# RWKV-7 recurrence of one layer: state and read-out products in 64x64 tiles of both heads, decayed state added on VectorE, scores and tokens of two blocks issued together

## The chip, the cores and the metric

The program runs on one core of one Trainium2 chip. The metric is the device time of one execution in microseconds. Three runs of the kernel before gave 1727.79, 1728.28 and 1729.55 us, median 1728.28.

## The reference

One layer of a streaming encoder on 1024 tokens of width 1024: a mixing stage (8 heads of latent attention beside 8 heads of RWKV-7), a memory cross-attention with 256 memory tokens, a squared-ReLU MLP of width 4096 and a last RMSNorm, all in float32. The change touches the RWKV-7 recurrence alone. Per head (64 channels) and token the reference does:

```python
def step(state, inp):
    rt, wt, kt, vt, at, bt = inp
    sa = jnp.einsum('bhvk,bhk->bhv', state, at)
    state = state * wt[:, :, None, :] + sa[..., None] * bt[:, :, None, :] + vt[..., None] * kt[:, :, None, :]
    return state, jnp.einsum('bhvk,bhk->bhv', state, rt)
```

After it each head is normalised, a bonus term sum(r k r_k) v is added and a gate multiplies the result. The rates w, a and the gate come from low-rank products of the projected input.

## The kernel before

**Stages.** The execution runs the input projection, attention with pieces of other work between its heads (to about 442 us), then the recurrence loop (first solve at 463.25, last output at 717.0 us), then the memory values, the output projection, cross-attention and the MLP, which are long rows of full matmuls. Every stage is written out as one instruction order per engine, with semaphores (`Steps` objects name each event) between the engines. A wait holds up all that stands behind it on its engine.

**The recurrence loop.** Heads go in pairs: channels of head 0 of the pair on partitions 0 to 63, of head 1 on 64 to 127. A round is one pair (`p`, 0 to 3). The 1024 tokens are 16 chunks (`c`) of 64, two chunks are a block (`w`, 8 of them), two blocks a group (`g`, 0 to 3 in a round). In a group TensorE does, for its own two blocks: `solve` (L1361), the inverse of the chunk's triangular system times two right sides, gives P and G; `local` and `other_r` (L1372, L1411) give what a chunk reads from itself and its matrix for reading the state; `carry` (L1418) gives the matrix by which the state moves over a chunk, to which VectorE adds the diagonal decay (`mt`, L2748) that GpSimd built as diagonal matrices (`dg`, L902). Then, for k = 0 to 3, `state` (L1437, copied out by VectorE at L2758) and `outputs` (L1449) of one chunk each. `state` and `outputs` contract over 128 partitions: the state with an identity under it, and the transition matrix with the additive part under it, so that each is one 128-row, 64-column product per head (L1445, L1458).

Between these stand, for the next group: the doubling of the inverse (`double_q` L1334 for k = 0 and 2, `double_z` L1347 for k = 1 and 3, masked or added by VectorE at L2721 and L2730), `scores` of one block for k = 0 and 1 (L1290, masked by VectorE at L2604), `tokens` of one block for k = 2 and 3 (L1312: three 128x128 transposes and one 128x128 product, copied by ScalarE at L1941 to L1944), and after k = 3 `a_v` of both blocks (L1325, copied at L1949).

**Work beside it.** `beside(p, s)` puts slot `s` of 44 per round into the order: `prep(p+1, s)` makes the next round's inputs and `post(p-1, s-22)` finishes the last round's output. Group g has slots 11g+4 to 11g+6 before k = 0 and two slots for each k (11g+7+2k and the next; the first before and the second after `scores` or `tokens`). Slots that matter here, with their lines:
- 0 to 3: four low-rank products on TensorE (L1208), each followed by a tanh on ScalarE (L1882, L1886), all through one PSUM bank; slot 3 also has three VectorE passes.
- 5 to 7: squares on ScalarE (L1892), two block sums on TensorE (L1211), each followed by a logarithm (L1897).
- 10, 11: exponentials W, kf and Wi on ScalarE (L1903, L1905, L1908). 14 to 17: VectorE passes nkk (L2512, which needs kf), at (L2517), b and bt (L2522, L2526), kt (L2529).
- 18, 19: products `al` (L1256), masked by VectorE (L2539), which SyncE stores to DRAM and loads back as 16x16 blocks (L689, L693).
- 26 to 30: 15 substitution steps on those blocks, two small VectorE instructions each (L2562, L2565), then `xt` (L2568), stored and loaded again for the inverses.
- 28, 29 and 37 to 39: the statistics and the gate of the round before (L1211, L1208, L2588 to L2598). 33, 34: the bonus sums (L1211, L2574).

Slots 0 to 3 of the next round fall after k = 2 and 3 of group 3. In round 3 there is no next round, and ScalarE and VectorE prepare the memory tokens instead (L1976 to L2000, L2632).

## Time and profile before

| what | value |
|---|---|
| three runs | 1727.79, 1728.28, 1729.55 us |
| profiled execution, its own time | 1724.08 us |
| its span, first to last instruction | 1722.0 us |
| mean granted TensorE clock | 0.985 |
| busy share: TensorE, VectorE, ScalarE, GpSimd | 96%, 65%, 51%, 45% |
| recurrence loop, first solve to last output | 463.25 to 717.0 us |

The span is the time between the first and the last instruction on the core; the execution's own time has 2.1 us around it. A TensorE row of the timeline merges neighbouring instructions of one line; its duration runs from the first start to the modelled end of the last. A float32 product shows as two matmul instructions, a transpose as one. PEclk is the granted clock, 1.00 for 2.4 GHz and 0.50 for 1.2 GHz.

### The profile page before, as it was taken

To read this page: it belongs to the slowest core of one execution; us is meant where nothing else is said; L and a number is where in the kernel's file an instruction comes from. 1 tells how busy PE (TensorE), PEld (TensorE's weight loads), DVE (VectorE), ACT (ScalarE), POOL (GpSimd) and SP (SyncE) were. 2 spreads that over 40 slices of the span, in tenths; PEclk is the share of its full clock that TensorE was granted. 3 is DMA by queue.
4 is the path that set the end of the run, shared out by engine and by line. 5 is a ranking of instruction groups with operands and counts; after the bars stand their busy time and mean duration, and the time that the engine had idled before them with its cause. 6 is when DMAs were issued, how large, how long until landed. Compare 5 with 4: busy or idle time off the path is not lost.

```text
span 1722.0 us, 30291 instructions
## 1 busy us (share of the span) xinstructions
PE 1653.9 (96%) x11840; PEld 1272.0 (74%) x11840; DVE 1115.8 (65%) x1728; ACT 869.9 (51%) x1687; POOL 768.4 (45%) x555
## 2 busy tenths in 40 slices
PE   8999999998989888899999999999999999999997
PEld 6676777745666667688977667788888888888886
DVE  7744343435576675633687769887758866784788
ACT  5323333345334444611453467776667566666763
POOL 4120212011111122313393257968768695867771
PEclk9999999979899999999999999999999999999999
DMA  6010010001121214332302003020212202120202
GB/s 241 25 37 22 25 47 1 22 6 31 33 36 42 53 24 128 136 110 73 111 25 74 1 1 98 19 80 26 74 30 69 72 28 92 31 74 25 74 1 98
DMA packets 82841, 94.45 MB, mean 55 GB/s; under 512 B 53776, under 2 KB 56336, under 8 KB 82704
## 3 DMA queue, kind: packets, MB, share of 16 engines
q1 hardware_dynamic: 82704, 92.56, 17.3%
q8 instruction: 93, 1.52, 0.4%
q14 instruction: 44, 0.36, 0.1%
HBM read 82.57 MB, written 9.98 MB: 54 GB/s over the span
## 4 chain that ended last, share of the span: by engine, by line
PE 79%; DVE 10%; ACT 4%; issue 3%; DMA 2%; POOL 2%; SPq 0%; DVEq 0%; ACTq 0%; POOLq 0%
PE PS L1707 41%; PE PS L1034 8%; PE PS L969 5%; PE PS L1135 3%; PE PS L1174 2%; PE PS L1153 2%; PE PS L1208 2%; PE PS L1663 2%; PE PS L1641 1%; PE PS L1211 1%; PE PS L1499 1%; POOL sa L917 1%; PE PS L1343 1%; DMA sc_s<-a_dram 1%; PE PS L1445 1%
## 5 line engine op out<-in xcount | busy, mean ns | idle before, releaser
L1707 PE MATMUL PS<-memr,wsp 128*128 128x512 f32 x1488 | 358.3, 391 | 1.0 <-DVE memr L2877 1.0
L1707 PEld LDWEIGHTS PS<-memr,wsp 128*128 128x128 f32 x1488 | 278.8, 188 | 63.7 <-DVE memr L2877 3.0
L932 POOL TENSOR_TENSOR wsp<-sa,wsp 128x512 fp32r<-128x512 f32 x120 | 167.5, 1399 | 166.0 <-ACT wsp L2135 165.8
L1707 PE MATMUL PS<-memr,wraw_r 128*128 128x512 f32 x744 | 180.5, 391 | 0.0
L1707 PEld LDWEIGHTS PS<-memr,wraw_r 128*128 128x128 f32 x744 | 139.4, 188 | 30.9 <-DVE memr L2877 0.6
L1707 PE MATMUL PS<-tmp_r,wsp 128*128 128x512 f32 x564 | 148.3, 397 | 2.5 <-DVE tmp_r L2877 2.2
L2877 DVE TENSOR_TENSOR memr<-PS,memr 128x512 fp32r<-128x512 f32 x185 | 126.1, 682 | 34.9 <-ACT PS L2173 34.6
L1034 PE MATMUL PS<-xn,wsp 128*128 128x512 f32 x576 | 147.5, 403 | 0.9 <-DVE tmp L2350 0.7
L969 PE MATMUL PS<-xn,wsp 128*128 128x512 f32 x576 | 132.5, 391 | 5.0 <-DVE xn L2313 3.7
L2895 DVE TENSOR_TENSOR H<-PS,H 128x512 f32<-128x512 f32 x160 | 108.1, 686 | 44.7 <-PE PS L1707 28.0
L823 POOL CAST wsp<-wraw 128x1024 fp32r<-128x1024 f32 x24 | 26.5, 1106 | 240.1 <-PE PS L1034 115.9
L1034 PEld LDWEIGHTS PS<-xn,wsp 128*128 128x128 f32 x576 | 105.6, 190 | 33.8 <-issue 13.8
L1842 ACT ACTIVATE H<-PS,mst 128x128 f32<-128x128 f32 (+3 forms) x64 | 47.4, 741 | 164.2 <-DVE mst L2442 164.2
L969 PEld LDWEIGHTS PS<-xn,wsp 128*128 128x128 f32 x576 | 107.8, 188 | 29.8 <-issue 4.9
L1707 PEld LDWEIGHTS PS<-tmp_r,wsp 128*128 128x128 f32 x564 | 105.4, 188 | 29.7 <-DVE tmp_r L2877 4.0
L2164 ACT CAST memr<-sa 128x512 fp32r<-128x512 f32 x114 | 70.2, 616 | 109.7 <-PE PS L1707 80.0
L932 POOL TENSOR_TENSOR wraw_r<-sa,wraw_r 128x512 fp32r<-128x512 f32 x64 | 89.0, 1394 | 53.5 <-ACT wraw_r L2135 53.5
L917 POOL TENSOR_TENSOR sa<-sa 128x512 f32<-128x512 f32 x64 | 91.7, 1434 | 34.9 <-DMA sa<-in_weights_dram 33.0
L2173 ACT COPY PS<-sa 128x512 f32<-128x512 f32 x175 | 101.9, 582 | 3.2 <-DVE con_r L2877 1.8
L2442 DVE TENSOR_REDUCE mst<-PS 128x1 f32<-128x128 f32 (+3 forms) x64 | 48.1, 753 | 85.1 <-PE PS L1138 85.0
L932 POOL TENSOR_TENSOR wsp<-sbx,wsp 128x512 fp32r<-128x512 f32 x66 | 88.6, 1345 | 11.9 <-ACT wsp L2135 11.8
L2821 DVE TENSOR_TENSOR sa<-sa 128x512 f32<-128x512 f32 x80 | 88.4, 1108 | 6.6 <-ACT sa L2114 6.6
(382 smaller groups left out, 3393.2 us busy)
## 6 DMA issues: line engine op xcount, KB each, us to landing
sa<-in_weights_dram SPq DMA_DIRECT2D x40, 512.0 KB, 4.3
wraw<-in_weights_dram SPq DMA_DIRECT2D x24, 512.0 KB, 3.8
sa<-in_weights_dram SPq DMA_DIRECT2D x48, 256.0 KB, 2.8
H<-in_x_dram SPq DMA_DIRECT2D x16, 512.0 KB, 7.7
sbx<-in_weights_dram SPq DMA_DIRECT2D x32, 256.0 KB, 2.9
H<-in_weights_dram SPq DMA_DIRECT2D x8, 512.0 KB, 7.3
out_dram<-sbx SPq DMA_DIRECT2D x16, 256.0 KB, 2.1
a_dram<-H SPq DMA_DIRECT2D x16, 128.0 KB, 2.5
```

What stands on the lines that cost most here:

```text
L917: nc.gpsimd.tensor_tensor(out, a, b, op).then_inc(W_SUM.sem, W_SUM.one(name))
L932: nc.gpsimd.tensor_tensor(w[:, 1, :], w_source(g), w[:, 0, :].bitcast(F32), ALU.subtract).then_inc(mw_rest, 1)
L969: last = nc.tensor.matmul(PS[:, bank + half, :], wsp[:, k, kt, a, :], src[:, at, b, HALF * half:HALF * half + HALF], start=(i == 0 and (a, ...
L1034: last = nc.tensor.matmul(PS[:, bank, :], wsp[:, u % 2, kt, a, :], xn[:, kt, b, HALF * half:HALF * half + HALF], start=(kt == 0 and (a, b) ...
L1135: nc.tensor.matmul(PS[:, b + part, 0:n], mQ[:, win(q)], mK[:, HALF * part:HALF * part + n], start=True, stop=(part < q // 4))
L1707: last = nc.tensor.matmul(PS[:, bank_of(g), :], w[:, a, win(k)], x[:, b, :], start=(k == 0 and (a, b) == (0, 0)), stop=(k == ROWS - 1 and ...
L2164: nc.scalar.copy(x_split_of(d)[:, 0, :], x_source(d)).then_inc(mx_head, 1)
L2173: nc.scalar.copy(PS[:, PS_BANKS + d % 2, :], x_source(d)).then_inc(mx_staged, 1)
L2442: m(nc.vector.tensor_reduce(mNeg[h % 2][:, q:q + 1], two(2 * (q % 2))[:, 0:P * (q + 1)], AX_X, ALU.max, negate=True), f"m{h}_{q}")
L2821: nc.vector.tensor_tensor(out, a, b, op).then_inc(X_SUM.sem, X_SUM.one(name))
L2877: nc.vector.tensor_tensor(x[:, 1, :], source, x[:, 0, :].bitcast(F32), ALU.subtract).then_inc(mx_rest, 1)
L2895: out(nc.vector.tensor_tensor(tile, a, b, ALU.add), f"{kind}{part}_{v}")
```

## The change

Head h of a pair keeps to partitions 64h to 64h+63 all through the recurrence. The state is one tile of 128x64 for each chunk (both heads, no identity under it), the transition matrix has no diagonal and no additive part, and both `state` and `outputs` are 64x64 products, one for each head. The additive part goes straight into the PSUM bank of the new state with `given` (four 64x64 products for each chunk, issued one chunk ahead), and `state` adds its product to it. VectorE then makes the new state with one scalar_tensor_tensor: old state times the chunk's decay (a column for each channel) plus the PSUM tile. GpSimd's diagonal matrices, the `mt` addition on VectorE and the selection products `from_r` are gone: ScalarE copies the transition matrices (`mt`) and the local outputs (`ly`), VectorE adds r to the local reads (`r`) and the local outputs to the read-out (`y`), which ScalarE only copied before. Scores and tokens of both blocks of a group are issued together, for k = 0 and k = 1, with one masking instruction for both; the tokens are 32 products of 64x64 with the identity as moving operand instead of transposes; `a_v` comes for k = 2. Their ScalarE copies stand at the same places: four token copies between the two slots of k = 1, the `a_v` copy between those of k = 2. The setting up of the loop loses VectorE's 64x2048 identity copy and five memsets but one, and its filler products are placed differently. DMA issues are the same; some of SyncE's, GpSimd's and ScalarE's waits name the new events.

In the cut below the lines that it removes are left out (they are in the listing above), and of the new order of each engine what matters; 8 columns of indent are taken off.

```diff
@@ -1287,60 +1274,69 @@
...
+    def scores(p, g):
...
+        for s in range(2):
+            w, at = 2 * g + s, 192 * s
+            for h, c in QUADS:
+                rows = slice(HD * h, HD * h + HD)
+                nc.tensor.matmul(PS[chunk(c), h, at:at + CH], rB[i][rows, win(w)][:, chunk(c)],
+                                 rAR[i][rows, w, 1, chunk(c)], start=True, stop=True)
+            for h, c in QUADS:
+                rows = slice(HD * h, HD * h + HD)
+                last = nc.tensor.matmul(PS[chunk(c), h, at + CH:at + 3 * CH].rearrange("p (a n) -> p a n", a=2),
+                                        proj[rows, T_K + p, win(w)][:, chunk(c)], rAR[i][rows, w, :, chunk(c)],
+                                        start=True, stop=True)
+        last.then_inc(L_PE.sem, L_PE.one(f"sc{p}_{g}"))
+    def tokens(p, g):
+        i = p % 2
+        if g == 0:
             r_at(P_POOL, f"bh_{p}")
...
+        r_at(L_DVE, f"sc{p}_{g}")
+        for s in range(2):
+            w, at = 2 * g + s, 256 * s
+            for h, c in QUADS:
+                rows = slice(HD * h, HD * h + HD)
+                nc.tensor.matmul(PS[chunk(c), h, at + 192:at + 256], proj[rows, T_V + p, win(w)][:, chunk(c)],
+                                 con[rows, C_CV + HD * h:C_CV + HD * h + HD], start=True, stop=True)
+            for k, src in enumerate((rAR[i][:, w, 0, :], rBh[i][:, win(w)], rKh[i][:, win(w)])):
+                for h, c in QUADS:
+                    rows = slice(HD * h, HD * h + HD)
+                    last = nc.tensor.matmul(PS[chunk(c), h, at + CH * k:at + CH * k + CH],
+                                            src[rows, chunk(c)], ident[rows, rows], start=True, stop=True)
+        last.then_inc(L_PE.sem, L_PE.one(f"tok{p}_{g}"))
...
@@ -1350,114 +1346,84 @@
...
+    def quad(out, h, c, left, right, start, stop):
+        return nc.tensor.matmul(PS[HD * h:HD * h + HD, out[0], out[1]:out[1] + CH], left, right, start=start, stop=stop)
+    def cols(h):
+        return slice(HD * h, HD * h + HD)
+    def carry(p, g):
+        for s in range(2):
+            r_at(L_ACT, f"pg{p}_{2 * g + s}")
+            for h, c in QUADS:
+                quad((c, CH * s), h, c, rPG[s][chunk(c), h, 0:HD], rBKs[g % 2][chunk(c), s, 0, cols(h)], True, True)
+            for h, c in QUADS:
+                quad((c, P + CH * s), h, c, rPG[s][chunk(c), h, HD:P], rSC[s][chunk(c), h, 0, :], True, False)
+            for h, c in QUADS:
+                last = quad((c, P + CH * s), h, c, rVs[g % 2][chunk(c), s, h, :], rSC[s][chunk(c), h, 2, :], False, True)
+        last.then_inc(L_PE.sem, L_PE.one(f"mn{p}_{g}"))
+    def reads(p, g):
+        for s in range(2):
+            for h, c in QUADS:
+                last = quad((2 + c, CH * s), h, c, rPG[s][chunk(c), h, 0:HD], rSC[s][chunk(c), h, 0, :], True, True)
+        last.then_inc(L_PE.sem, L_PE.one(f"lr{p}_{g}"))
+    def given(p, c):
...
+        e = c // 4 % 2
+        for k, right in enumerate((rPG[s][:, :, HD:P], rVs[e][:, s])):
+            for h in range(2):
+                last = quad((5 - n, 0), h, n, rBKs[e][chunk(n), s, k, cols(h)], right[chunk(n), h, :], k == 0, False)
+        last.then_inc(L_PE.sem, L_PE.one(f"n{p}_{c}"))
     def state(p, c):
...
+        if c % 4 == 0:
+            r_at(L_ACT, f"mt{p}_{c // 4}")
+        r_at(L_PE, f"n{p}_{c}")
         if c >= 1:
             r_at(L_DVE, f"st{p}_{c - 1}")
...
         for h in range(2):
...
+            last = quad((5 - c % 2, 0), h, h, rMT[cols(h), c % 2, c // 2 % 2, :], rST[cols(h), c, :], False, True)
         last.then_inc(L_PE.sem, L_PE.one(f"st{p}_{c}"))
     def outputs(p, c):
...
+        if c % 4 == 0:
+            r_at(L_DVE, f"r{p}_{c // 4}")
         if c >= 1:
             r_at(L_DVE, f"st{p}_{c - 1}")
...
         for h in range(2):
...
+            last = quad((4 + c % 2, P + CH * (c // 2 % 2)), h, h, rST[cols(h), c, :],
+                        rR[cols(h), c % 2, c // 2 % 2, :], True, True)
+        last.then_inc(L_PE.sem, L_PE.one(f"o{p}_{c}"))
     def beside(p, s):
@@ -1577,33 +1546,26 @@
             for w in ab:
                 solve(p, w)
             beside(p, t + 4)
...
+            carry(p, g)
+            reads(p, g)
             beside(p, t + 5)
...
+            given(p, 4 * g)
             beside(p, t + 6)
             for k in range(4):
                 c = 4 * g + k
...
                 if c < NC - 1:
                     state(p, c)
...
+                outputs(p, c)
                 first, second = places(g, k)
                 if more:
                     for n in range(2):
                         (double_z if k % 2 else double_q)(k // 2, *following(p, g, n))
+                if k < 3 and c < NC - 2:
+                    given(p, c + 1)
                 beside(p, first)
...
+                if more and k < 3:
+                    (scores, tokens, a_v)[k](*group_after(p, g))
                 beside(p, second)
...
@@ -1934,20 +1894,19 @@
...
+    def tokens(p, g):
+        tok = PS[:, 0:2, :].rearrange("p h (s k n) -> p s k h n", s=2, k=4)
+        r_at(L_PE, f"tok{p}_{g}")
+        nc.scalar.copy(rVs[g % 2], tok[:, :, 3]).then_inc(L_ACT.sem, L_ACT.one(f"vz{p}_{g}"))
+        nc.scalar.copy(rAGs[:, :, :, 0:HD], tok[:, :, 0]).then_inc(L_ACT.sem, L_ACT.one(f"ag{p}_{g}"))
+        for s, name in enumerate(("ba", "bk")):
+            nc.scalar.copy(rBKs[g % 2][:, s].rearrange("p k (h n) -> p k h n", h=2), tok[:, s, 1:3]).then_inc(
+                L_ACT.sem, L_ACT.one(f"{name}{p}_{g}"))
...
@@ -2066,28 +2023,24 @@
             more = g < NW // 2 - 1 or p < PAIRS - 1
             for w in ab:
                 r_at(L_PE, f"pg{p}_{w}")
...
+                nc.scalar.copy(rPG[w % 2].rearrange("p h n -> p (h n)"), PS[:, 2 + w % 2, 0:256]).then_inc(
                     L_ACT.sem, L_ACT.one(f"pg{p}_{w}"))
             beside(p, t + 4)
...
+            r_at(L_PE, f"mn{p}_{g}")
+            nc.scalar.copy(rMT.rearrange("p c s n -> p c (s n)"), PS[:, 0:2, 0:P]).then_inc(
+                L_ACT.sem, L_ACT.one(f"mt{p}_{g}"))
+            if p or g:
+                r_at(L_DVE, f"y{p}_{g - 1}" if g else f"y{p - 1}_{NW // 2 - 1}")
+            nc.scalar.copy(rY.rearrange("p c s n -> p c (s n)"), PS[:, 0:2, P:2 * P]).then_inc(
+                L_ACT.sem, L_ACT.one(f"ly{p}_{g}"))
             beside(p, t + 5)
             beside(p, t + 6)
             for k in range(4):
                 first, second = places(g, k)
...
                 beside(p, first)
...
+                if more and k in (1, 2):
+                    (tokens, a_v)[k - 1](*group_after(p, g))
                 beside(p, second)
...
@@ -2741,30 +2687,39 @@
         for g in range(NW // 2):
             ab, t = (2 * g, 2 * g + 1), 11 * g
             more = g < NW // 2 - 1 or p < PAIRS - 1
...
+            beside(p, t + 4)
+            r_at(L_PE, f"lr{p}_{g}")
+            nc.vector.tensor_tensor(rR, PS[:, 2:4, 0:P].rearrange("p c (s n) -> p c s n", s=2),
+                                    rAR[p % 2][:, ab[0]:ab[0] + 2, 1, :].rearrange("p s (c n) -> p c s n", c=2),
+                                    ALU.add).then_inc(L_DVE.sem, L_DVE.one(f"r{p}_{g}"))
+            beside(p, t + 5)
             beside(p, t + 6)
             for k in range(4):
                 c = 4 * g + k
                 if c < NC - 1:
                     r_at(L_PE, f"st{p}_{c}")
...
+                    if c == 0:
+                        r_at(P_ACT, f"wt_{p}")
+                        dve.wait_ge(rp_dve, 2)
+                    else:
+                        r_at(L_DVE, f"st{p}_{c - 1}")
+                    nc.vector.scalar_tensor_tensor(rST[:, c + 1], rST[:, c], rWT[p % 2][:, c:c + 1],
+                                                   PS[:, 5 - k % 2, 0:CH], ALU.mult, ALU.add).then_inc(
                         L_DVE.sem, L_DVE.one(f"st{p}_{c}"))
                 first, second = places(g, k)
                 if more:
                     for n in range(2):
                         (added_z if k % 2 else masked_q)(k // 2, *following(p, g, n))
+                if k == 3:
+                    r_at(L_PE, f"o{p}_{c}")
+                    r_at(L_ACT, f"ly{p}_{g}")
+                    nc.vector.tensor_tensor(
+                        proj[:, T_R + p, 256 * g:256 * g + 256].rearrange("p (s c n) -> p c s n", s=2, c=2),
+                        PS[:, 4:6, P:2 * P].rearrange("p c (s n) -> p c s n", s=2), rY,
+                        ALU.add).then_inc(L_DVE.sem, L_DVE.one(f"y{p}_{g}"))
                 beside(p, first)
...
+                if more and k == 0:
+                    masked_scores(*group_after(p, g))
                 beside(p, second)
```

## Rows read from the trace of the kernel before

**Rows 1.** The page: its header and TensorE's busy time and share.
```profile
span 1722.0 us, 30291 instructions
...
PE 1653.9 (96%) x11840; PEld 1272.0 (74%) x11840; DVE 1115.8 (65%) x1728; ACT 869.9 (51%) x1687; POOL 768.4 (45%) x555
```

**Rows 2.** Busy time of stretches of the loop, with granted clock and DMA.
```profile
core 0: us, PE busy (x) PEld busy (x) DVE busy (x) ACT busy (x) POOL busy (x), PEclk, DMA share, GB/s
561.00:580.20 19.20, 17.01 (x314) 11.82 (x312) 14.51 (x50) 8.71 (x18) 2.99 (x5) 0.91 0.20 30
628.40:647.30 18.90, 15.72 (x314) 10.96 (x310) 14.10 (x50) 8.71 (x18) 2.92 (x5) 1.00 0.25 33
679.50:692.30 12.80, 11.32 (x306) 9.60 (x302) 8.20 (x21) 6.00 (x17) 5.44 (x4) 1.00 0.02 4
```

**Rows 3.** Timeline of TensorE: start, us, line, count, idle before.
```profile
463.25 1.97 PE L1368 MATMUL PS<-sc_s,H 64*64 64x128 f32 x16
...
600.97 0.70 PE L1425 MATMUL PS<-sc_s 64*64 64x64 f32 x26
...
603.74 0.34 PE L1458 MATMUL PS<-sc_s,tmp 128*64 128x64 f32 x4
...
604.23 0.68 PE L1343 MATMUL PS<-H 64*64 64x64 f32 x16
...
605.90 0.36 PE L1305 MATMUL PS<-sa 64*64 64x64 f32 x8
...
606.41 0.39 PE L1445 MATMUL PS<-tmp,ssum 128*64 128x64 f32 x3
...
609.50 0.33 PE L1318 MATMUL PS<-con,sa 128*128 128x128 f32 x1
609.66 0.27 PE L1319 MATMUL PS<-con,sa 128*128 128x128 f32 x1
...
612.87 0.45 PE L1330 MATMUL PS<-sc_s,sc_w 64*64 64x64 f32 x8 [0.42 <-ACT sc_s L1944]
613.15 1.19 PE L1368 MATMUL PS<-sc_s,H 64*64 64x128 f32 x16
...
620.14 1.15 PE L1256 MATMUL PS<-sa 64*64 64x64 f32 x32 [0.45 <-DVE H L2539]
```

**Rows 4.** Line L1425: shortest, median and longest ns of one instruction.
```profile
L1425 PE MATMUL PS<-sc_s x768: 218/218/267, 466.5 to 711.1; 64*64 64x64 f32 x192
```

**Rows 5.** The chain that ended last, inside round 2: start, us, what.
```profile
590.67 1.07 PE PS L1208 x2
...
596.39 1.14 PE PS L1208 x2
...
604.91 1.07 PE PS L1211 x2
...
606.62 1.28 ACT L1903
607.91 1.06 ACT sa L1903
608.97 0.94 ACT sa L1905
...
611.01 0.27 ACT sc_s L1942
...
611.62 1.23 DVE sa L2512
...
616.55 0.70 DVE ssum L2748
...
623.79 3.59 DMA a_dram<-H
...
639.57 0.38 DVE sc_s L2568
```

**Rows 6.** Timeline of VectorE: one masking of scores.
```profile
608.54 0.56 DVE L2604 TENSOR_TENSOR sc_w<-PS,con 128x384 f32<-128x384 f32 x1
```

More of the change, by code:

```diff
@@ L119 @@
 POST = 22
-RP_SET = 6
 SPLITS = ((10, 4), (14, 2))
@@ L1325, in a_v @@
[L1325 to L1332 removed]
+                if p or g:
+                    r_at(L_ACT, f"ly{p}_{g - 1}" if g else f"ly{p - 1}_{NW // 2 - 1}")
@@ L1334, in double_q, with a_v @@
+            def a_v(p, g):
+                r_at(L_ACT, f"bk{p}_{g}")
+                for h in range(2):
+                    for s in range(2):
+                        for c in range(2):
+                            last = nc.tensor.matmul(PS[chunk(c), s, HD * h:HD * h + HD], rSC[s][chunk(c), h, 1, :],
+                                                    rVs[g % 2][chunk(c), s, h, :], start=True, stop=True)
+                last.then_inc(L_PE.sem, L_PE.one(f"akv{p}_{g}"))
             def double_q(lv, p, w):
@@ L1404, in from_r @@
-            def from_r(p, w, h, c):
-                rows = slice(HD * h, HD * h + HD)
-                return nc.tensor.matmul(PS[0:HD, 2 + 2 * (w % 2) + c, CH * h:CH * h + CH],
-                                        con[rows, C_SEL + CH * h:C_SEL + CH * h + CH],
-                                        rAR[p % 2][rows, w, 1, chunk(c)], start=False, stop=(h != c))
-            def other_r(p, w):
-                r_at(L_PE, f"lo{p}_{w}")
-                for h in range(2):
-                    last = from_r(p, w, h, 1 - h)
-                last.then_inc(L_PE.sem, L_PE.one(f"ry{p}_{w}"))
@@ L1556, in attention_end @@
                     pair_factors(PAIRS - 1, s - 6)
-            for stage in (scores, tokens, a_v):
-                for w in range(2):
-                    if stage is scores and w or stage is tokens and not w:
-                        keep_busy(2 + w, 2 * P)
-                    stage(0, w)
-            pe.wait_ge(rp_dve, RP_SET)
+            scores(0, 0)
+            for bank in (2, 3):
+                keep_busy(bank, 2 * P)
+            tokens(0, 0)
+            keep_busy(4, HALF)
+            a_v(0, 0)
+            pe.wait_ge(rp_dve, 2)
             for bank in (2, 4, 3):
@@ L2055, in _ @@
                     values(h // 2 + 1)
[L2057 to L2060 removed]
+            tokens(0, 0)
+            a_v(0, 0)
             for s in range(4):
```

310 lines of the change are left out of this document (78 added, 232 removed).

## The prediction

> **What bounds the kernel now.** I read the page first: TensorE is busy 96% of a span of 1722.0 us [rows 1]. That share misleads in the loop, because a matmul's row lasts until its modelled end while the next ones already start. So I took the loop (254 us, 16 groups) by stretches [rows 2]: a group takes 12.8 us where nothing stands beside it and 19.2 where substitution does. Then the timeline of TensorE in round 2, for what each piece occupies from its start to the next start, and last the chain of waits in the same round, for what the next round's inputs need. The reader is to see that TensorE streams nearly without gaps, while a second chain (ScalarE, VectorE, DMA) runs just as long beside it. In round 2 it holds the end at four places [rows 5]:
> - slots 0 to 3, a product and a tanh in turn through one bank, 1.91 us each ((596.39-590.67)/3);
> - the block sum that ends at 605.98, the table load and exponentials (606.62 to 609.91), then four VectorE passes from 611.62 until `mt` at 616.55;
> - the trip of the blocks to DRAM and back from 623.79 and the substitution until 639.95;
> - TensorE for the rest, among it the 7.3 us from there to 647.3, where group 3 begins [rows 2].
>
> **TensorE, part by part.** In four quadrants an instruction costs (0.70-0.22)/25 = 19 ns [rows 3, 4]; on the two diagonal quadrants (0.68-0.22)/15 = 31 ns; with both column halves but one row half (L1256) (1.15-0.22)/31 = 30 ns [rows 3].
> - `state` and `outputs` of a chunk: 8 instructions, 0.49 us (603.74 to 604.23). As 64x64 on the diagonal: 8 x 30 ns = 0.24. Saves 0.25, 1.0 a group.
> - `local`, `other_r` and `carry`: 112 instructions a group become 64, all in four quadrants: saves 48 x 19 ns = 0.9.
> - `given`: 32 new instructions a group. No row shows it; between 19 ns and an unpipelined 218 [rows 4] the nearest is L1256, same row half, so 30 ns: adds 0.95.
> - scores: 0.51 a block now (605.90 to 606.41). Sorted by size, 8 x 19 + 8 x 28 (double columns) = 0.38: saves 0.25 a group.
> - tokens: three transposes and a product for a block come to 5 x 0.11 plus 0.05 for the change of mode (0.16 to the second transpose, then 0.11). 32 small instructions are 0.61. Even; 1.3 us a group either way.
> - `a_v`: its waits for the token copies (0.42 idle before L1330, beside 0.2 under the last row's end) go twice, 1.2 a group. `mt` no longer comes through VectorE: about 0.6.
>
> Together 3.0 us a group. If TensorE alone set the end, that would be 16 x 3.0 = 48 us. It doesn't.
>
> The Trainium skill speaks against `given`: by TensorE: Matmul & The Clock Gate (Part 3, What overlaps and what doesn't) a weight load overlaps a running matmul only when its row group differs, and `given` keeps to one row half. Row L1256 does the same and still runs at 30 ns, so the sum keeps that price; by the rule `given` would run one by one (a rival below).
>
> **The other engines.** VectorE loses `mt` (0.70 [rows 5]) and gets `r` and `y`, 128x256 from PSUM; between a masking of 128x384 (0.56 [rows 6]) and zero, by their third less columns, 0.4 each. The two maskings become one of double width: 2 x 0.56 less one fixed part of 0.16 = 0.96. The new state by scalar_tensor_tensor, 0.25 for a copy of 0.27. Even. ScalarE copies fewer and wider, 0.27 each for 256 columns [rows 5]. GpSimd loses 32 instructions that nothing waited long for; their absence is costed at nothing, under the `carry` products. SyncE issues the same DMAs.
>
> **What moves, round 2 walked through.** The price is in the order on ScalarE. Token copies stood after slots 10 and 11; now they stand before slot 10, and they wait for all token products.
> 1. The squares of slot 5 start once `carry` is copied: 0.9 less of products and one wait for products less (estimated 0.15), so 1.05 earlier. The block sum of slot 7 ends at 604.93 instead of 605.98.
> 2. TensorE then does scores 0.8, a chunk 0.25, doubling 0.95, `given` 0.25, tokens 1.3: 608.5. Four copies: 609.6. Only now the table load and exponentials, 1.28+1.06+0.94: kf at 612.9, before at 609.91. **3.0 later.**
> 3. Wi (0.95) and the `a_v` copy behind it end at 614.1. `solve` of group 1 starts there, 1.0 later than 613.15, after some 3 us in which TensorE has nothing.
> 4. VectorE starts nkk at 612.9 instead of 611.62, ends `at` at 615.4, and now meets `r`, which waits for `solve` 1.1, copy 0.3, half of `carry` 0.5 and `reads` 0.35: 616.4. Then 0.4, and b and bt 2.46: 619.3 instead of 616.55. **2.8 later.**
> 5. kt (1.23), new state and maskings stand before the masking of `al` as before; the second `al` is ready 1.9 later and the blocks leave 1.8 later than 623.79.
> 6. DMA unchanged. The substitution loses `mt` and gets `r`: -0.5. It ends 1.3 late, at 641.3.
> 7. From there to `solve` of group 3 took 7.3. Now addition 0.75, doubling 0.6, `given` 0.25, block sum, addition and block sum 2.9, a chunk 0.25, doubling and addition 0.95: 5.7, `solve` at 647.0. Round 2 has won 0.3; past the gate products 0.55.
> 8. Inside group 3, from k = 0 to slot 0 of the next round, TensorE did three chunks, three doublings and two scores: 1.47+2.2+1.02 = 4.7. Now it does three chunks 0.72, doublings 2.2, three `given` 0.75, scores 0.8 and all tokens 1.3: 5.8. Slots 0 to 3 keep their 1.91 each; the gap that tokens filled stays open. Net **+0.55** for a round that hands over to another with preparation.
>
> Sum: setting up the loop -0.5 (VectorE's identity copy no longer there; the filler products pace it). Round 0 +1.0: the same walk with a smaller gain in step 1 (pair sums of the attention stand there too). Round 1 +0.55. Round 2 -1.0: no slots 0 to 3 follow, and `a_v` waits no more. Round 3: no preparation, but in its group 0 the `a_v` copy stands behind a logarithm and an exponential with a table load of 1.28 each [rows 5] and a cast, so -1.2 only; groups 1 and 2 -1.3 each of 3.0, since VectorE's scaling and casts now stand ahead of the state; the last about +0.1. So -3.7. Total -3.65 us. The later stages wait for the loop through TensorE and shift with it. Against the profiled execution's own 1724.08 that is 1720.4; the runs' median lies 4.2 above it, so **1724.6**.
>
> **Rivals.**
> - **TensorE's gain gets through.** If ScalarE is not late at step 2 (table loaded while it waits, tokens sooner), steps 2 to 5 lose nothing, and outside the fixed parts (slots 0 to 3 6.9, DMA and substitution 18.7 with `al`, of 66 us) each of three rounds gains up to 3.0/16 of 40 us, some 7, and round 3 up to 9: -30. Half of it, -15, is the likelier value: 1713. For it: the stalls before L1330 and `mt` are on the chain in every group [rows 3]. Against it: the orders as written, and DMA and substitution that no product shortens. Chance 0.27.
> - **Slower, through the clock.** The 3 us without work at step 3 (and some 2 before group 2's `r`) let the granted clock fall. Group 2 of round 1 is at 0.91 already [rows 2], and `solve` at 463.25 took 1.97 against 1.19 [rows 3]. Halved speed in `solve`, `carry` and `reads` adds 2 us at step 4, in three rounds 6, at group 2 and in round 3 another 4: +6, 1734. It decides once the clock falls in more than one of the three. Chance 0.22.
> - **`given` one by one.** 60 calls x (8 x 0.218 - 0.24) = +90 at most [rows 4]. Chance 0.02.
>
> **Numbers.** Forecast case 0.49, within 4 us of its value either way, split about evenly by the bound of 0.2% (3.5 us, about what a measurement of this kernel can tell from no change). Faster: 0.27 and half of 0.49, 0.51. Slower: 0.24. Same: 0.25. The 8 in 10 go from 1706 (most of the first rival) to 1735 (most of the second). The forecast case alone: 1720 to 1729.
>
> **What would show it.** Right: tokens of group 1 copied on ScalarE just before the table load of L1903's counterpart, kf about 3 us later after the block sum than 3.9; idle of some 3 us before `solve` of group 1 put down to the `a_v` copy; `state` and `outputs` 0.24 a chunk; `given` 0.24; TensorE's busy time in the loop down by 20 us or more while the loop shortens by under 6; period of rounds 0 and 1 unchanged within 1.5 us. Wrong: rounds shorter by 4 us or more, exponentials that start before the token copies, `given` above 0.5, or a clock below 0.9 over whole rounds.

## The result, and the profile after

The changed kernel takes **1743.01 us** (median of 4 runs, 1733.11 to 1751.49) beside 1728.03 for the kernel before (4 runs, 1724.95 to 1729.55): ratio 1.009, 95% interval 1.0063 to 1.0116. It is slower by 15 us, on the other side of the forecast (1724.6) and above the range's upper end of 1735. Run once more on another occasion it gave 1740.93 (6 runs), ratio 1.0083 (1.0058 to 1.0107). One run of the kernel with kf ahead of W, 1856.77 us at a granted clock of 0.835, is left out of all that follows. The profiled execution of the change is the fastest of its four, 1733.11 with a span of 1731.3; so its rows show only part of the loss. Its header and busy times, to be read against [rows 1]:

```profile
span 1731.3 us, 31351 instructions
...
PE 1632.3 (94%) x12418; PEld 1262.1 (73%) x12418; DVE 1112.0 (64%) x1724; ACT 858.6 (50%) x1619; POOL 746.3 (43%) x523
```

TensorE lost 21.6 us of work (1653.9 to 1632.3), and the span grew by 9.3. The loop from first solve to last output (busy time by engine, granted clock, DMA share), before the change:

```profile
463.25:717.30 254.05, 224.28 (x4919) 171.66 (x4919) 169.62 (x410) 116.78 (x275) 50.41 (x46) 0.98 0.24 61
```

and after it, with the stretches that answer to [rows 2]:

```profile
core 0: us, PE busy (x) PEld busy (x) DVE busy (x) ACT busy (x) POOL busy (x), PEclk, DMA share, GB/s
463.35:725.20 261.85, 203.66 (x5442) 162.23 (x5442) 166.01 (x410) 105.12 (x212) 28.70 (x15) 0.93 0.24 61
...
566.57:586.88 20.31, 15.63 (x345) 10.82 (x345) 12.43 (x52) 8.27 (x15) 1.62 (x1) 0.92 0.22 29
635.75:655.47 19.72, 15.62 (x345) 10.82 (x345) 12.43 (x52) 8.28 (x15) 1.27 (x1) 0.91 0.20 23
687.89:700.81 12.92, 10.47 (x337) 9.85 (x337) 7.49 (x21) 5.42 (x14) 3.40 (x2) 0.88 0.02 4
```

TensorE's busy time in the loop fell from 224.3 to 203.7 us, what is left of the loop rose from 30 to 58. The granted clock is the second difference: 0.93 for 0.98. By rounds, the first three took 72.1, 69.4 and 63.3 us (67.9, 67.3 and 62.9 before); the fourth, to the start of the last output, 56.5 (55.7); what follows takes 1.8 more.

The timeline of TensorE in round 2, against [rows 3]:

```profile
604.83 1.09 PE L1364 MATMUL PS<-sc_s,H 64*64 64x128 f32 x16
...
608.69 1.12 PE L1198 MATMUL PS<-sa,con 128*128 128x512 f32 x2 [1.26 <-ACT sa L1854]
...
616.54 0.59 PE L1324 MATMUL PS<-sc_s,sc_w 64*64 64x64 f32 x14
...
620.95 1.09 PE L1364 MATMUL PS<-sc_s,H 64*64 64x128 f32 x16 [3.06 <-ACT sc_s L1908]
...
642.79 0.33 PE L1370 MATMUL PS<-sc_s,tmp 64*64 64x64 f32 x4 [3.13 <-DVE sc_s L2692]
```

Two stalls stand out: 3.06 us before `solve` of group 1 (L1364), ended by the `a_v` copy (L1908), and 3.13 before the first outputs of group 2, ended by `r` (L2692). The `a_v` products themselves (L1324) had started at 616.54. The first returns in all four rounds (3.14, 3.14, 3.06, 3.34), and in rounds 1 and 3 `solve` behind it took 1.97 us, the length at 1.2 GHz, for 1.09. The chain of waits through the same place, against [rows 5] (start, us, what):

```profile
610.89 1.06 PE PS L1198 x2
...
614.74 0.30 PE PS L1314 x22
615.45 0.38 ACT sc_s L1901
615.82 0.55 ACT ssum L1903 x2
616.39 1.28 ACT L1865
617.69 1.06 ACT sa L1865
618.75 0.95 ACT sa L1867
619.69 0.95 ACT sa L1870
620.64 0.27 ACT sc_s L1908
620.95 1.09 PE PS L1364 x16
...
632.77 3.94 DMA a_dram<-H
636.73 3.78 DMA sc_s<-a_dram
```

The order is the predicted one: token products (L1314), token copies (L1900 to L1903), only then the table load and the exponentials W, kf and Wi (L1865 to L1870), then the `a_v` copy, then `solve`. From the block sum's end at 611.95 to the table load, 4.4 us, ScalarE has only a logarithm of 0.6 us and 1.2 us of copies to do; for 2.6 us it waits for the token products. One more thing follows from the order. The product on GpSimd (L853) starts when W is there, and nkk on VectorE (L2465) when kf is there, so that the two run side by side:

```profile
618.82 2.35 POOL L853 TENSOR_TENSOR sa<-proj,sa 128x1024 f32<-128x1024 f32 x1 [50.64 <-ACT sa L1865]
```

```profile
619.72 2.53 DVE L2465 SCALAR_TENSOR_TENSOR sa<-sa 128x1024 f32<-128x1024 f32 x1 [1.17 <-ACT sa L1867]
```

nkk takes 2.53 us in all three rounds; in the kernel before it starts after GpSimd's product has ended and takes 1.23 [rows 5]. The masking of both blocks' scores answers to [rows 6], 0.96 as predicted:

```profile
612.85 0.96 DVE L2556 TENSOR_TENSOR sc_w<-PS,con 128x768 f32<-128x768 f32 x1 [1.85 <-PE PS L1294]
```

### The profile page after: what moved, and what is told of

The parts are those of the page before. It is cut to its first block, busy times and chain, and to the rows that moved or that the text cites. A ratio compares the mean times of both kernels' runs of the same rounds, so it can differ in the third digit from the quotient of the medians.

```text
span 1731.3 us, 31351 instructions
## 1 busy us (share of the span) xinstructions
PE 1632.3 (94%) x12418; PEld 1262.1 (73%) x12418; DVE 1112.0 (64%) x1724; ACT 858.6 (50%) x1619; POOL 746.3 (43%) x523
## 4 chain that ended last, share of the span: by engine, by line
PE 77%; DVE 13%; ACT 4%; issue 3%; DMA 2%; SPq 0%; DVEq 0%; ACTq 0%
PE PS L1669 40%; PE PS L1021 8%; PE PS L956 5%; PE PS L1122 3%; PE PS L1161 2%; PE PS L1140 2%; PE PS L1195 2%; PE PS L1370 2%; PE PS L1625 2%; PE PS L1603 1%; PE PS L1467 1%; DVE sa L2776 1%; PE PS L1198 1%; DMA sc_s<-a_dram 1%; PE PS L1364 1%
## 5 line engine op out<-in xcount | busy, mean ns | idle before, releaser
L2850 DVE TENSOR_TENSOR H<-PS,H 128x512 f32<-128x512 f32 x160 | 108.2, 687 | 44.8 <-PE PS L1669 27.8
```

Source lines behind the costliest of these rows:

```text
L2850: out(nc.vector.tensor_tensor(tile, a, b, ALU.add), f"{kind}{part}_{v}")
```

## The experiments

Twelve kernels. Each ratio is to runs of the kernel before on the same chip (median 1728.0 beside the first row, 1725.5 to 1726.5 beside the others). "Clock" is the median over the runs of the mean granted clock; the kernel before has 0.983.

| kernel | median us | ratio (95% interval) | clock |
|---|---|---|---|
| the change | 1743.01 | 1.009 (1.0063 to 1.0116) | 0.966 |
| the change again | 1740.93 | 1.0083 (1.0058 to 1.0107) | 0.968 |
| exponentials first | 1726.27 | 1.0012 (0.9994 to 1.0029) | 0.974 |
| exponentials and `a_v` copy first | 1736.99 | 1.0056 (1.0035 to 1.0077) | 0.972 |
| idle filled, order kept | 1736.64 | 1.0063 (1.0044 to 1.0081) | 0.975 |
| `r` first in group 2 | 1743.86 | 1.010 (1.0076 to 1.0124) | 0.966 |
| exponentials first, group 2 filled | 1725.03 | 0.9998 (0.9984 to 1.0012) | 0.975 |
| the same, group 1 filled too | 1725.29 | 0.9993 (0.9978 to 1.0007) | 0.978 |
| all of it, `a_v` copy early in group 0, end filled | 1722.75 | 0.9985 (0.9971 to 0.9999) | 0.981 |
| the same with kf ahead of W | 1723.09 | 0.998 (0.9967 to 0.9994) | 0.980 |
| before, exponentials late | 1741.89 | 1.0089 (1.0072 to 1.0107) | 0.980 |
| before, group 2 filled | 1724.28 | 0.9994 (0.9985 to 1.0003) | 0.985 |
| before, filled, kf ahead of W | 1726.67 | 1.0007 (0.9997 to 1.0018) | 0.984 |

**Order or clock.** Two theories stood after the first reading: the place of the exponentials on ScalarE behind the token copies costs (order theory), or TensorE's waits cost through the clock that they let fall (clock theory). The first four kernels split them. Exponentials first, on ScalarE alone:

```diff
                         beside(p, first)
-                        if more and k in (1, 2):
-                            (tokens, a_v)[k - 1](*group_after(p, g))
+                        if more and k == 2:
+                            a_v(*group_after(p, g))
                         beside(p, second)
+                        if more and k == 1:
+                            tokens(*group_after(p, g))
```

> The change with one edit: ScalarE's four token copies stand behind slot 10 (exponentials W and kf) instead of ahead of it; the a_v copy stays behind slot 11. Nothing else moves. If the order on ScalarE is what costs (theory 1): in rounds 0 to 2 the exponentials start as soon as the logarithm of slot 7 is done, kf ends some 2.7 us earlier after the start of its round, the second masking of al 2.5 us earlier, the idle before solve of group 1 falls from 3.1 to about 1.7 us, and three rounds gain 2 us each and round 3 about 1: the median falls from 1743.0 to about 1736. If the clock is what costs (theory 2), the idle stretches before solve and before the first outputs of group 2 stay above 1.5 us, as many windows at 1.2 GHz are seen in the loop, and the median stays within 3 us of 1743.

It took 1726.27 us, 15 to 17 below the change by the medians and 12 to 14 by the ratios, where the order theory asked for 7. The timeline of its ScalarE in round 2, and one row of its VectorE:

```profile
610.19 1.06 ACT L1865 ACTIVATE sa<-sa 128x1024 f32<-128x1024 f32 x1
611.15 1.04 ACT L1867 ACTIVATE sa<-sa 128x1024 f32<-128x1024 f32 x1
612.10 0.35 ACT L1900 COPY sc_s<-PS 128x256 f32<-128x256 f32 x1
...
614.10 0.39 ACT L1908 COPY sc_s<-PS 128x256 f32<-128x256 f32 x1
```

```profile
615.30 1.22 DVE L2467 SCALAR_TENSOR_TENSOR sa<-sa 128x1024 f32<-128x1024 f32 x1
```

The round began at 600.14, so kf (L1867) ends 12.1 us into it for 14.9 in the change, the `a_v` copy (L1908) starts 14.0 into it for 15.7, and `solve` of group 1 starts at 14.8 without the wait of 3 us. But nkk (L2467) starts 15.2 into the round, no earlier than in the change (14.9): it stands behind VectorE's `y`, not behind kf. So an earlier start through kf is not there. The second chain gains behind it: from the start of nkk to the end of the last masking of `al` it is 9.6 us for 11.3. Most of that, 1.3 us, is nkk itself, 1.22 us for 2.53, since GpSimd's product (started 11.2 us into the round, 2.36 us long) has ended by then; the rest is `r`, which comes with `solve`.

The other kernel kept the order and filled the idle time:

```diff
+            def hold(n):
+                for _ in range(n):
+                    nc.tensor.matmul(PS[:, 4, 2 * P:HALF], con[:, 0:P], con[:, 0:2 * P], start=True, stop=True)
...
+                    if g == 1:
+                        r_at(L_DVE, f"y{p}_0")
+                        hold(5)
                     for w in ab:
                         solve(p, w)
...
                             state(p, c)
+                        if g == 2 and k == 0 and p < PAIRS - 1:
+                            hold(6)
                         outputs(p, c)
```

> The change with idle time filled and no order touched: five products of 128x128 by 256 columns with no reader before solve of group 1 (in the idle of 3.1 us, once y of group 0 is there) and six before the first outputs of group 2 (in the idle of some 3 us). 38 products, some 0.43 us each, 16 us of TensorE work that lies in waits. Clock theory: mean granted clock rises from the 0.962 to 0.978 seen in four runs to 0.98 or more, the windows at 1.2 GHz in the loop become fewer than half, the median falls by 7 us or more to 1736 or below, and the runs lie closer together than the 18 us of before. Order theory: the waits stand as they are, so the time falls by 2 us at most; where fillers overrun their wait it rises.

1736.64: 4 to 6 us below the change at a clock of 0.975. The five products overran their wait (group 0 took 18.4, 17.0 and 17.1 us for 18.0, 16.1 and 16.1, 2.3 us in all), so the clock is worth somewhat more than that. Group 2 of round 1 took 17.59 us at full clock for 20.31. Neither theory alone: filling gives a third of what the order gives.

**Two that failed.**

```diff
-                    beside(p, t + 4)
+                    if g != 2:
+                        beside(p, t + 4)
                     r_at(L_PE, f"lr{p}_{g}")
...
+                    if g == 2:
+                        beside(p, t + 4)
```

> The change with one edit: in group 2 VectorE's addition r stands ahead of slot 26 (whose substitution waits for the blocks from DRAM) instead of behind it. The idle of 3 us of TensorE before the first outputs of group 2 goes in rounds 0 to 2. If that wait is on the path, 2 us a round: 1737. If what follows is set by VectorE, which still makes the substitution steps of slots 26 to 28 ahead of the first new state, nothing is won by it as a wait (within 1.5 us), unless the clock holds better because TensorE no longer stands still for so long (1 to 3 us by the clock theory).

1743.86, no gain, with the clock still at 0.966. The wait of TensorE before the first outputs of group 2 is gone from this kernel's trace, but TensorE waits later in the group instead, 5.3, 3.7 and 4.4 us in rounds 0 to 2. The wait itself is not on the path: VectorE comes to the first new state behind most of the substitution in any case (at 656.00 in round 2, with the substitution begun at 650.20).

```diff
+                        if more and k == 2:
+                            a_v(*group_after(p, g))
                         beside(p, first)
```

> As the kernel with the exponentials first, and the a_v copy of k = 2 also ahead of slot 11 (exponential Wi, in group 0) instead of behind it. Order theory: Wi has 2.5 us of slack behind kf (nkk and at on VectorE come first), so nothing is lost there, and solve of group 1 starts another 0.7 to 1.0 us earlier in each round (round 3: a table load, an exponential and a cast no longer stand ahead of the copy, 1.5 to 2 us): 3 us below the kernel with the exponentials first, about 1733. If instead VectorE sets the time from kf on in rounds 0 to 2, only round 3 gains: 1 to 2 us.

1736.99, 11 us above the kernel with the exponentials first, where 3 below were expected. `solve` of group 1 in round 2 did start earlier (13.84 us into the round). But the edit stood in every group, and in group 3 it put the copy, which waits for TensorE, ahead of slot 0's tanh of the next round. Groups 3 took 21.8, 19.6 and 14.1 us (18.3, 19.1 and 12.6 with the exponentials first). That this costs the 11 us is not shown. The first of the three, 3.5 of the 5.5 us, met a clock of 0.76, and a later kernel without this order in group 3 (kf ahead of W) took 23.9 us there at a clock of 0.73. What speaks for it is that the version below, which moves the copy in group 0 alone (and has products without a reader), does not lose.

**The same order in the old tiles.** If order is what costs, it must cost without the change:

```diff
-                        beside(p, first)
+                        late = g == 0 and p < PAIRS - 1
+                        if not (late and k == 2):
+                            beside(p, first)
                         if more and k >= 2:
                             tokens(*following(p, g, k - 2))
-                        beside(p, second)
+                        if late and k == 2:
+                            beside(p, first - 1)
+                            beside(p, first)
+                        if not (late and k == 1):
+                            beside(p, second)
```

> The kernel before the change, with one order on ScalarE turned the other way: in group 0 of rounds 0 to 2 the exponentials W and kf (slot 10) stand behind the token copies of k = 2 instead of ahead of them; no tile, product or buffer is changed. kf then waits for the first block's tokens: products until about 610.6 in round 2, copies until 611.3, table load and exponentials 3.28, so 614.6 for 609.91, 4.7 us later. Order theory (the time of the change comes from the place of the exponentials, whatever the tiles): three rounds lose 3 to 4 us each and the clock falls more often, 1738 to 1745. If it is the tiles and their clock that cost, this kernel loses by the walk alone what VectorE's chain cannot take up, 5 us at most, with its mean clock still at 0.98.

1741.89, 15.4 above its own before, with the clock at 0.980 for 0.983. Where it goes, TensorE's row in round 2 and the windows of groups 0 and 1 show:

```profile
627.66 0.45 PE L1330 MATMUL PS<-sc_s,sc_w 64*64 64x64 f32 x8 [4.08 <-ACT sc_s L1944]
```

```profile
core 0: us, PE busy (x) PEld busy (x) DVE busy (x) ACT busy (x) POOL busy (x), PEclk, DMA share, GB/s
609.58:627.95 18.37, 13.24 (x303) 10.15 (x305) 10.23 (x20) 11.32 (x23) 3.52 (x3) 1.00 0.01 2
627.95:644.50 16.55, 14.78 (x369) 13.03 (x367) 12.56 (x27) 4.86 (x15) 3.19 (x2) 0.90 0.16 35
```

A wait of 4.08 us in each of three rounds before the `a_v` products (0.42 in the kernel before); group 0 is longer by 4.0, 3.7 and 3.7 us, group 1 by 1.1 to 1.3, the rounds by 5.9, 4.1 and 5.6. A wait at this place passes whole to the end of the round. nkk, again beside GpSimd's product, takes 2.53 us here too. It is the same order in kind and not in size: kf ends 15.9 us into round 2 for 11.5 before, 4.4 later, where the change has 3.4.

**Order right, clock held.** To the kernel with the exponentials first, the six products ahead of group 2's first outputs were added, and in the second kernel two more:

```diff
                         outputs(p, c)
+                        if g == 1 and k == 0 and p < PAIRS - 1:
+                            hold(2)
```

> The same with the six products of group 2 alone. If group 2 is the place that costs, as good as with both, 1719 to 1722; if group 1 (granted clock 0.79 to 0.89 in rounds 0 and 1 with the exponentials first) carries as much, 1722 to 1724, and the run with both is 2 us or more below it; if neither costs, 1726.

> The change with the exponentials first and eight products without a reader a round (0.43 us each): six before the first outputs of group 2 and two behind the first outputs of group 1, where TensorE waits 1.4 us for bt. The kernel with the exponentials first alone ran at 0.973 to 0.978 and 1726.3 us; filling group 2 brought groups 2 and 3 to a full clock and took 2.7 us off group 2 in the change itself. If the clock still costs there: 0.980 or more and 1718 to 1721, below both kernels. If the clock only follows the waits and costs nothing of its own: 1725 to 1728.

1725.03 and 1725.29: about 1 us below the exponentials first alone by the medians, 2 to 3 by the ratios, whose intervals overlap, where up to 7 and 5 to 8 were expected. The windows of groups 1 and 2 in round 1, first without, then with the two products:

```profile
544.37:560.80 16.43, 14.04 (x401) 13.20 (x401) 13.18 (x26) 3.62 (x11) 2.22 (x2) 0.79 0.16 35
560.80:578.96 18.16, 16.99 (x357) 12.24 (x357) 12.42 (x52) 8.38 (x15) 1.60 (x1) 1.00 0.25 32
```

```profile
544.56:558.79 14.23, 12.80 (x404) 11.12 (x405) 12.85 (x26) 3.61 (x11) 2.20 (x2) 1.00 0.18 40
558.79:578.70 19.91, 17.05 (x356) 12.23 (x357) 12.41 (x52) 8.39 (x15) 1.63 (x1) 1.00 0.23 29
```

Two products of 0.43 us keep group 1 at full clock and make it 2.2 us shorter. Group 2 gives 1.75 of it back. Its length is set by the trip of the blocks and the substitution, not by TensorE: TensorE reached group 2 3.4 us earlier in the round, but the last masking of `al` came 2.5 us earlier and the trip took 9.4 us for 8.5, so that the substitution came 1.65 us earlier. Work saved on one of two chains of nearly equal length is mostly lost again in a wait for the other: that is the shape of this whole case.

**A version below both.** The `a_v` copy ahead of slot 11 in group 0 only, and products without a reader in the last group of round 3:

```diff
+                        if more and k == 2 and g == 0:
+                            a_v(*group_after(p, g))
                         beside(p, first)
+                        if more and k == 2 and g > 0:
+                            a_v(*group_after(p, g))
                         beside(p, second)
...
+                        if p == PAIRS - 1 and g == 3:
+                            hold(1 + k // 3, 2 if k == 3 else 4 + k % 2)
```

> The change with the exponentials first, the products without a reader behind group 1's first outputs (two) and ahead of group 2's (six), and two edits more: in group 0 alone the a_v copy stands ahead of slot 11 on ScalarE (in the kernel that moved it in every group, the copy of group 3 also stood ahead of slot 0's tanh, and groups 3 took 21.8, 19.6 and 14.1 us where the exponentials first alone gave 18.3, 19.1 and 12.6); and in the last group of round 3, where the granted clock was 0.87 to 0.94 and is 1.00 in the kernel before, one such product a chunk and two behind the last. If slot 0 is what made that kernel slow: solve of group 1 starts 0.7 us earlier in three rounds and 1.5 us earlier in round 3, the clock behind the loop stays at 1.00 (2 us), together 1720 to 1722, below the kernel before. If the a_v copy ahead of Wi is bad of itself (it delays bt), 1730 or more.

1722.75, ratio 0.9985: below the kernel before by 2.5 to 3.4 us; the interval ends at 0.9999, so just outside the noise. The loop and the 30 us behind it:

```profile
466.27:714.90 248.63, 212.75 (x5496) 168.55 (x5495) 161.94 (x409) 105.33 (x212) 29.61 (x15) 0.96 0.25 64
714.90:744.90 30.00, 30.00 (x127) 23.47 (x126) 16.84 (x13) 15.05 (x17) 8.65 (x4) 1.00 0.53 198
```

The loop is 248.6 us for 254.1 before and 261.9 in the change. In this trace it starts at 466.27, 3 us later than before; over the 14 profiles it starts from 461.2 to 466.3 (463.3 to 465.5 with the old tiles), so that spans of single profiles tell little about 3 us. TensorE's row is still empty for 36 us of the loop, more than before (30), with some 12 us of products without a reader counted as busy.

```diff
                         if k == 0:
                             outputs(p, c)
+                        if g == 2 and k == 0 and p < PAIRS - 1:
+                            for _ in range(4):
+                                nc.tensor.matmul(PS[:, 2, 2 * P:HALF], con[:, 0:P], con[:, 0:2 * P], start=True, stop=True)
```

> The kernel before with four products without a reader (0.43 us each) behind the first outputs of group 2 in rounds 0 to 2, where TensorE waits 1.5 to 2.5 us for mt. It tells whether filling helps the old tiles as well. Its clock in group 2 is 0.91 in rounds 0 and 1 and 1.00 in round 2: by the clock theory 1 to 3 us below the kernel before; if it only follows the waits, the same within 1 us, or slower by what overruns.

Four products behind the first outputs of group 2 in the old kernel: 1724.28, ratio 0.9994 (0.9985 to 1.0003). The interval holds 1: up to half of what the best version wins may be had without new tiles, but it is not shown.

In the last pair, slot 10 on ScalarE is turned round, with a wait of `at` for W on VectorE:

```diff
-                    nc.scalar.activation(rW, rWi, ACT.Exp, scale=-half_e).then_inc(sem_, one("W"))
                     r_at(P_ACT, f"kl1_{n}")
                     nc.scalar.activation(rB[i], rB[i], ACT.Exp, scale=-0.5).then_inc(sem_, one("kf"))
+                    nc.scalar.activation(rW, rWi, ACT.Exp, scale=-half_e).then_inc(sem_, one("W"))
```

> The version that did best so far (exponentials first, products without a reader, a_v copy early in group 0) with kf ahead of W in slot 10: kf is done 1.06 us earlier, nkk (1.22 us) starts with it, and at, the first that needs W, finds it ready. If the chain kf, nkk, at, b, bt, al, DRAM and back, substitution sets the length of a round now that TensorE has slack, three rounds gain 1.0 us each: about 1720. If TensorE sets it, the same 1722.7.

> The kernel before, with the four products without a reader behind the first outputs of group 2, and kf ahead of W in slot 10 as well, so that the old tiles get the same two helps. TensorE has less slack in the old tiles (28.8 us idle in the loop, against 56.8), so if the two chains are nearly equal there, the 1.0 us a round is worth less: 1723 to 1724. If it is worth the whole, 1721, and the new tiles are worth nothing against it.

kf ahead of W wins nothing clear of the noise: 1723.09 after 1722.75 (0.998 after 0.9985), and 1726.67 after 1724.28 in the old tiles. That agrees with the row of nkk above: once the exponentials are first, kf is done 3 us before VectorE comes to it. In the old tiles VectorE comes to nkk 13.2 us into rounds 1 and 2 with either order, and with kf first W is later, and with it GpSimd's product: it runs into the first 0.8 us of nkk, which takes 1.89 us for 1.22. With these helps in both, the new tiles are at 0.998 and the old at 1.0007, intervals apart; how much of that is nkk (0.7 us in each of three rounds) and how much the tiles was not tried.

And the change unchanged:

> The change itself once more, on the same chip as the two beside it. By the four runs so far: 1733 to 1751, median 1743, about 0.3 us more for each us more at 1.2 GHz (the clock's mean 0.978 to 0.962). If those four were a chance, it comes out at 1735 or below; the order theory alone (walk, full clock) would have 1728.

1740.93 and a profile at 1740.13, clock 0.967. It is the better picture of a typical run of the change. Its groups 0 and 1 in round 1:

```profile
534.13:551.12 16.99, 12.52 (x342) 10.43 (x341) 10.17 (x20) 11.26 (x19) 2.13 (x1) 0.90 0.01 3
551.12:566.99 15.87, 13.82 (x401) 13.00 (x401) 12.82 (x24) 3.68 (x12) 2.45 (x3) 0.78 0.17 36
```

## Why the prediction was wrong

The steps that failed are the sizes of the rounds in the sum, and behind them stand two prices. The late `a_v` copy was priced at 1.0 us at step 3 and the late exponentials at 1.8 at step 5, both won back by step 7; and the forecast case had nothing for the clock that the waits let fall, nor for nkk running beside GpSimd's product. The round terms were +1.0, +0.55, -1.0 and -3.7, -3.15 us together; the trace of the fastest run has +4.2, +2.1, +0.4 and +0.8, +7.5 together. The setting up of the loop (-0.5) gave +0.1, and 1.8 came behind the loop, for which the sum had no term. The median lies 10 us above that run.

**The walk, against the trace.** Offsets in us from the start of round 2 (598.44 before and in the forecast, 604.83 after):

| step | before | forecast | measured |
|---|---|---|---|
| 1. block sum of slot 7 ends | 7.5 | 6.5 | 7.1 |
| 2. tokens copied | | 11.2 | 11.5 |
| 2. kf done | 11.5 | 14.5 | 14.9 |
| 3. `solve` of group 1 | 14.7 | 15.7 | 16.1 |
| 4. bt done | 18.1 | 20.9 | 21.8 |
| 5. blocks leave | 25.4 | 27.2 | 27.9 |
| 6. substitution ends | 41.5 | 42.9 | 44.8 |
| 7. `solve` of group 3 | 48.8 | 48.6 | 50.6 |
| end of round | 62.9 | 61.9 | 63.3 |

What was right. The prices, by three pieces of the chain in round 2:

```profile
605.95 1.29 PE PS L1370 x64
...
612.78 0.22 PE PS L1370 x8
...
613.93 0.17 PE PS L1370 x6
```

`carry` and `reads` are 64 instructions of 20 ns for 19; `state` and `outputs` of a chunk 0.22 us for 0.24; `given` (the last row, six of its eight) 28 ns each for 30. The trace bears out the row taken as nearest, and that rival is out. The Trainium skill's rule in TensorE: Matmul & The Clock Gate, Part 3, What overlaps and what doesn't, would have had `given`, in one row half, run one by one; the trace, with 28 ns an instruction, does not agree. TensorE's busy time fell by the 20 us named. The order on ScalarE, kf 3.4 us later in the round for 3.0, the idle of 3 us before `solve` of group 1, from `k` = 0 of group 3 to slot 0 5.8 for 5.8 (before round 2), the substitution shorter by 0.5: all there.

What was wrong, step by step:

- **Step 1**: the squares start once the copies of carry and local outputs are done; they came 0.4 earlier, not 1.05.
- **Step 4**: nkk was priced at the 1.22 us of the row before. It took 2.53, beside GpSimd's product: with kf late, VectorE waits for it and the two start 0.9 us apart (that the one slows the other is read from coincidence in time; last section). This is 1.3 us in each of three rounds, and more than the 0.9 by which step 4 misses; the walk had no term for what else runs then.
- **Step 6, "DMA unchanged"**: from the last masking of `al` to the first substitution step it took 8.1, 9.8 and 9.5 us in the three rounds, before 7.8, 7.8 and 8.3. This is 1.3 of the 2.0 us by which steps 6 and 7 miss in round 2. Its cause is open (last section).
- **Round 3, -3.7**: the largest term of the sum, and not there; +0.8 was measured. Group 0 took 19.8 us for 18.2, where -1.2 was forecast: the table loads ahead of the `a_v` copy gave the wait of 3.34. `solve` behind it ran at 1.2 GHz, and groups 1 and 3 had clocks of 0.88 and 0.86. Group 2, at full clock, gained 1.35 for the 1.3 forecast.
- **Rounds 0, 1 and 2, +1.0, +0.55 and -1.0**: measured +4.2, +2.1 and +0.4. Of the 6.1 us that they miss, nkk is 3.9 and the longer trips of the blocks (step 6) 3.5; what the clock cost and what other steps won lie in the same sum and are not told apart. The forecast case had no term for the clock in any round.
- **The clock as a rival** was a part of the mechanism, with its place (the idle at step 3) and its point (more than one round) as named, but with 0.22 of the chance and priced at +6, 1734. Filling the waits, which raised the clock to 0.975 and left the order, gave back 4 to 6 of the 15 us. The profiled run came out there (1733.1); the others did not. Over the four runs the mean clock is 0.978, 0.966, 0.965 and 0.962 and the time 1733, 1742, 1744 and 1751. As 2 x (1 - clock) x span that is 76 to 133 us at 1.2 GHz, so 18 us over 57: 0.3 us for each. I priced half speed only in `solve`, `carry` and `reads`; it also fell on groups 1, 2 and 3 and on the stages behind the loop.
- **Step 3 as a price**: I let the late `a_v` copy cost 1.0 us and win back in group 1. The order turned in the old tiles shows that such a wait passes whole to the round's end, and more: 3.7 us more of wait, 4.1 to 5.9 us more of round.
- **"TensorE's gain gets through"** was the rival with 0.27. Its condition (ScalarE not late at step 2) was made true by the exponentials first: 1726.27, +0.1% and not 1713. With the clock held as well it is 1722.75. Filling alone gave the old kernel 1.8 (within the noise), so the new tiles themselves may be worth 1 to 2 us here, an estimate. TensorE's 20 us of saved work turned into idle time: its row is empty for 58 us of the loop in the change, for 30 before.

The sum of it: from the change to the exponentials first it is 15 to 17 us by the medians. The median time at 1.2 GHz falls from about 120 to 90 us with it; at 0.3 us each that is some 9. The rest, 6 to 8, is the waits and the slower nkk; 1.3 us in three rounds, some 4, would be nkk. That split is an estimate, and the 9 is its upper end: filling took about as much off the time at 1.2 GHz (120 to 87 us) and gave 4 to 6, with the 2.3 of overrun 7 to 9. That the order sets off the whole loss is shown by undoing it (1.0012), and that the same order costs as much in the old tiles by the kernel that has it (1.0089). Through which of the three (wait, clock, nkk) it costs how much is not shown.

## What to carry to other kernels

When products are packed tighter, look at which copies now wait for the last of them, and what stands behind those copies on the same engine: merging two blocks' tokens put a table load and three exponentials behind a wait, and that order cost some 15 us with either kind of tile. Keep work whose inputs are ready ahead of copies that wait for TensorE, but decide it for each group: moving the `a_v` copy forward in every group lost 11 us, moving it in one did not. Look also at what a later start brings side by side: nkk took twice its time beside GpSimd's product. Work taken off TensorE left waits in which its clock fell, and a profile that is the fastest of its runs hides this; compare the clock of all runs before the rows of one.

## What the runs showed of the hardware

- Two products of 128x128 by 256 columns (0.43 us each) in group 1 of round 1 were the difference between a granted clock of 0.79 and 1.00 there, 16.4 and 14.2 us. With them group 1 ran at 1.00 in all nine rounds profiled; with the exponentials first and no such products at 0.79 to 0.89 in seven rounds of nine, and at 1.00 in two.
- The kernel with the old tiles and the exponentials late bore waits of 4.08 us at a clock of 0.980, the change fell to 0.966 with waits of 3.1. It also has more of them: 18 waits of TensorE over 1 us in the loop, 39.5 us together, against 10 and 22.6 us. And the old group has transposes of 128x128 and products over 128 rows where the new one has 64x64. Which of the two is why was not tried.
- VectorE's nkk (128x1024, both inputs and the output in SBUF) took 2.52 to 2.54 us in the 15 profiled rounds in which it started 0.9 us after GpSimd's product of the same size, 1.21 to 1.22 us in the 24 in which that product had ended, and 1.89 in the 3 in which they overlapped for 0.8 us. No kernel moves the GpSimd product alone, so this is shown by coincidence in time.
- The trip of the blocks (four stores and a load of 128 KB each, from the last masking of `al` to the first substitution step) took 7.1 to 8.3 us in the 12 rounds profiled with old tiles, mean 7.6, and 7.4 to 10.6 in the 30 with new ones, mean 8.9. Queue orders are the same. Issuing the four stores took 2.7 us in all 12 and 2.7 to 3.8 in the 30; the rest of the difference lies in the landing of the last store and in the load. It makes some 4 us a run and stays open.
